# Router in column tiles, choosing experts by rank, first gather from plain rows, bias rows in two rounded passes

## The reference, cut to what matters

```python
scores = softmax(xt @ w_router + b_router)             # first block
grp = scores.reshape(-1, 4, 4)
g_sel = argmax(sum(top_k(grp, 2)))                     # best group by its two best experts
top_w, top_i = top_k(grp[g_sel], 2)
top_w = top_w / sum(top_w)
y = sum_e gate[:, e] * ((silu(xt @ w_gate[e]) * (xt @ w_up[e])) @ w_down[e])
# second block: aff = sigmoid(h @ router_w); the choice is made on aff + router_b,
# the two weights are aff[chosen] / sum(aff[chosen])
```

## Time and profile before

| | |
|---|---|
| runs | 1913.51, 1915.91, 1916.86 us (median 1915.91) |
| profiled execution | 1918.07 us, span from the first to the last instruction 1916.3 us |
| PE | 1750.4 us busy, 91% of the span |
| DVE, ACT | 771.9 us (40%), 403.3 us (21%) |
| weight transfers by SP | 500.20 MB, 299 GB/s read over the span |
| granted TensorE clock, mean | 0.948 of 2.4 GHz |
| chain that ended last | PE 72%, DMA 15%, DVE 7% |

### The profile page before, as it was taken

How to read it: one execution, slowest core, us unless ns; L and a number is a source line. 1 busy time by engine, 2 the same in 40 slices (tenths; PEclk the granted TensorE clock), 3 DMA queues, 4 the chain that set the end, 5 groups by cost and what they waited for, 6 DMA issues and landing times.

```text
span 1916.3 us, 21027 instructions
## 1 busy us (share of the span) xinstructions
PE 1750.4 (91%) x8248; PEld 1032.9 (54%) x8248; DVE 771.9 (40%) x1684; ACT 403.3 (21%) x760; POOL 87.6 (5%) x136
## 2 busy tenths in 40 slices
PE   8999989989799998899897999799998888899995
PEld 4587754433457777544336876544443664654342
DVE  1688631211356766222116356431221654412223
ACT  1232221111022232111103454111110441111111
POOL 1112000000110110000000000000000100000000
PEclk9999969999899998899998999799999899699998
DMA  9868569999974866599995512387999642388995
GB/s 378 338 242 324 220 213 417 421 422 421 421 304 150 316 250 258 230 422 421 421 424 205 215 50 95 126 325 285 421 421 423 241 167 89 150 342 342 421 421 242
DMA packets 82317, 574.46 MB, mean 300 GB/s; under 512 B 8736, under 2 KB 12832, under 8 KB 26912
## 3 DMA queue, kind: packets, MB, share of 16 engines
q1 hardware_dynamic: 60624, 500.20, 64.3%
q0 software_dynamic: 15264, 59.78, 8.4%
q10 hardware_dynamic: 6320, 12.99, 1.9%
HBM read 569.78 MB, written 3.15 MB: 299 GB/s over the span
## 4 chain that ended last, share of the span: by engine, by line
PE 72%; DMA 15%; DVE 7%; issue 3%; ACT 2%; SPq 0%; POOL 0%; POOLq 0%; ACTq 0%; DVEq 0%
PE bank L747 70%; DMA ring<-in_weights 11%; DMA hi_ring<-in_weights 3%; PE bank L779 2%; DVE work L1779 1%; DVE mix L1921 1%; ACT work L1370 1%; DMA consts<-in_cst 1%; DVE mix L1779 1%; DVE small L1779 1%; ACT mix L1370 0%; PE bank L875 0%; DVE oT L1957 0%; DVE small L1930 0%; ACT xT L1370 0%
## 5 line engine op out<-in xcount | busy, mean ns | idle before, releaser
L747 PE MATMUL bank<-ring,work 128*64 128x512 f32 (+2 forms) x1516 | 390.6, 584 | 24.5 <-DMA ring<-in_weights 23.1
L1370 ACT ACTIVATE work<-bank 128x512 f32<-128x512 f32 (+8 forms) x227 | 121.8, 538 | 866.8 <-PE bank L747 467.3
L747 PEld LDWEIGHTS bank<-ring,work 128*64 128x64 f32 (+2 forms) x1516 | 141.5, 144 | 253.4 <-issue 244.0
L747 PE MATMUL bank<-ring,oT 128*64 128x512 f32 (+1 forms) x864 | 228.7, 615 | 8.2 <-DMA ring<-in_weights 7.9
L1779 DVE TENSOR_TENSOR work_parts<-bank,work_parts 128x512 fp32r<-128x512 f32 x68 | 47.0, 692 | 371.8 <-ACT work_parts L1370 371.8
L747 PE MATMUL bank<-hi_ring,work 128*64 128x512 f32 (+1 forms) x608 | 154.3, 596 | 7.5 <-DMA hi_ring<-in_weights 6.0
L747 PEld LDWEIGHTS bank<-ring,oT 128*64 128x64 f32 (+1 forms) x864 | 77.9, 149 | 141.7 <-issue 141.6
L747 PE MATMUL bank<-work_parts 128*128 128x512 f32 (+2 forms) x592 | 147.7, 359 | 5.0 <-DVE work_parts L1779 5.0
L2121 DVE SCALAR_TENSOR_TENSOR work<-bank,small,work 128x512 f32<-128x512 f32 x34 | 25.5, 751 | 308.5 <-PE bank L747 244.4
L747 PE MATMUL bank<-ring,xT 128*128 128x512 f32 (+2 forms) x352 | 138.0, 550 | 1.8 <-DVE xT L2260 1.8
L747 PEld LDWEIGHTS bank<-work_parts 128*128 128x128 f32 x592 | 104.7, 204 | 54.4 <-issue 38.6
(11 more groups left out here) (233 smaller groups left out, 2170.3 us busy)
## 6 DMA issues: line engine op xcount, KB each, us to landing
ring<-in_weights SPq DMA_DIRECT2D x244, 1024.0 KB, 15.1
hi_ring<-in_weights SPq DMA_DIRECT2D x118, 1024.0 KB, 16.2
ring<-in_weights SPq DMA_DIRECT2D x52, 2048.0 KB, 10.2
hi_ring<-in_ada POOLq DMA_DIRECT2D x38, 512.0 KB, 11.4
mod_rows<-in_ada POOLq DMA_DIRECT2D x25, 512.0 KB, 5.9
work<-in_ada POOLq DMA_DIRECT2D x22, 512.0 KB, 6.4
hi_ring<-in_weights SPq DMA_DIRECT2D x5, 2048.0 KB, 10.6
work<-in_vecs POOLq DMA_DIRECT2D x8, 1024.0 KB, 6.4
```

What stands on the lines that cost most here:

```text
L747: ins = nc.tensor.matmul(o, lhsT, rhs, start=start, stop=stop)
L1370: return nc.scalar.activation(o, i, f, **kw)
```

## The change

Five edits:

- **Router.** The logits are computed the other way round: 32 columns of weights (16 and 16 zeros) fixed, 256 columns of `xT` moving, four column tiles side by side (`o[rows, 0:S]`, chunk c in tile c % 4). ACT copies the bank to `router_sums`, and two plain products with `stack` add the four partial sums and turn them. The weights of layers `e` and `o` are loaded over the first ones by a DMA of ACT in layer `1`. In `e` and `o` ACT takes the exponential straight from the bank, and `gate_rows` moves behind `gate_up("u", 0)`.
- **Choosing experts.** All pairs within a group are compared at once (128 elements a row): an expert's rank is how many of its group beat it. The softmax isn't normalised, since only ratios are used.
- **Ranks in rounded form.** `r_in`, `before` and `ones` are rounded (0, 1 are exact), so that the rank products are one record each; the totals are a product of their own, `count`, read by DVE after `picks(0)`.
- **First gather from plain rows.** `gather(0)` takes plain `x` (or `mix`) and plain `pick`: 16 plain products in place of 32 rounded ones. `src_low` moves behind `gathered(0)` and `positions`; `places(0)` moves behind `gate(0)`; ACT's `scaled` moves behind the exponential.
- **Bias rows** are 16 rounded products (table in a high and a low part) in place of 8 plain ones; DVE makes the parts before the cross-attention of layer 0.

```diff
@@ PE, experts @@
-                every = cs("ones")[:, 0:1].broadcast_to([P, P])
+                every = ones_parts[:, 0:1].broadcast_to([P, P])
                 product(f"{tag}.rank", [
-                    (0, NEXP, P, [(cs("before"), r_in[:, 0, :])]),
-                    (NEXP, 2 * NEXP, P, [(every, r_in[:, 0, :]), (cs("before"), r_in[:, 1, :])]),
-                    (2 * NEXP, 3 * NEXP, P, [(every, r_in[:, T, :]) for T in range(NT)])])
+                    (0, NEXP, P, [(before_parts, r_in[:, 0, :])]),
+                    (NEXP, 2 * NEXP, P, [(every, r_in[:, 0, :]), (before_parts, r_in[:, 1, :])])])
+                product(f"{tag}.count", [(0, NEXP, P, [(every, r_in[:, T, :]) for T in range(NT)])])
@@ PE, gather @@
-                                        [(src[:, T, (c0 + c) * P:(c0 + c + 1) * P], pick_parts[:, T, 0:width])
-                                         for src in (src_hi, src_lo(tag)) for T in range(NT)]) for c in range(per)])
+                                        [(src[:, T, (c0 + c) * P:(c0 + c + 1) * P], to[:, T, 0:width])
+                                         for src in rows for T in range(NT)]) for c in range(per)])
...
                 gather(0)
+                gate(0)
                 places(0)
-                gate(0)
                 gate_up("u", 0)
+                if between:
+                    between()
                 gather(1)
@@ PE, bias_rows @@
-                    product(f"row.{h}", [(0, UROW, P, [(pr("rel_table")[0:33, h:h + 1].broadcast_to([33, P]),
-                                                        cs("onehot")[0:33, :])])])
+                    product(f"row.{h}", [(0, UROW, P, [(rel_parts[0:33, k, h:h + 1].broadcast_to([33, P]), onehot_parts[0:33, :])
+                                                       for k in range(2)])])
@@ PE, route @@
-                wr = pr(weights, DC, 16)
-                product(name, [(T * 16, (T + 1) * 16, P, [(xT[:, c, T * P:(T + 1) * P], wr[:, c, :])
-                                                         for c in range(DC)]) for T in range(NT)])
+                wr = pr("router", DC, 32)
+                o = begin(f"{tag}.part")
+                for c in range(DC):
+                    rows = slice(32 * (c % 4), 32 * (c % 4 + 1))
+                    ins = mm(o[rows, 0:S], wr[:, c, :], xT[:, c, :], c < 4, c >= 4)
+                end(f"{tag}.part", ins)
+                ready(f"{tag}.part")
+                product(f"{tag}.logits", [(T * 16, (T + 1) * 16, P, [(router_sums[:, T * P:(T + 1) * P], cs("stack"))])
+                                          for T in range(NT)])
@@ layers e and o (PE; ACT alike) @@
-            route("e.logits", "router_w_2")
-            gate_rows("e.gf", sm("modc", 2, 48)[:, 0, 40:48])
-            experts("e.moe")
+            route("e")
+            experts("e.moe", lambda: gate_rows("e.gf", sm("modc", 2, 48)[:, 0, 40:48]))
@@ ACT @@
                 turned(turn)
+                whole(router_sums, f"{tag[0]}.part")
                 src_high(tag, 1, NT * n + 2)
-            act.wait_ge(router_in, 3)
-            fn(rA, rA, ACT.Exp, scale=-1.0).then_inc(router_exp, 1)
+            whole(ro("A"), "e.logits", ACT.Exp, scale=-1.0)
@@ DVE, route: the thirty small steps become @@
+                other, own = (four.unsqueeze(k).broadcast_to([P, 8, 4, 4]) for k in (2, 3))
+                step.later(tt(r_beats, other, own, ALU.is_gt))
+                step(tt(r_equal, other, own, ALU.is_equal))
+                step(tt(r_equal, r_equal, cs("earlier", 4, 4).unsqueeze(1).broadcast_to([P, 8, 4, 4]), ALU.mult))
+                step(tt(r_beats, r_beats, r_equal, ALU.add))
+                step(v.tensor_reduce(r_rank, r_beats, AX.X, ALU.add))
+                step(v.scalar_tensor_tensor(out=r_top, in0=r_rank, scalar=1.5, in1=four, op0=ALU.is_lt, op1=ALU.mult))
+                step(v.tensor_reduce(r_score.rearrange("p t g -> p (t g)"), r_top, AX.X, ALU.add))
+                step(v.tensor_reduce(r2a, r_score, AX.X, ALU.max))
+                step(tt(r_g, r_score, r2a.unsqueeze(2).broadcast_to([P, 2, 4]), ALU.is_equal))
+                step(tt(r_g, r_g, cs("rank4").unsqueeze(1).broadcast_to([P, 2, 4]), ALU.mult))
+                step(v.tensor_reduce(r2a, r_g, AX.X, ALU.max))
+                step(tt(r_g, r_g, r2a.unsqueeze(2).broadcast_to([P, 2, 4]), ALU.is_equal))
+                v.scalar_tensor_tensor(
+                    out=r_in.rearrange("p t (g j) -> p (t g) j", g=4), in0=r_rank, scalar=1.5,
+                    in1=r_g.rearrange("p t g -> p (t g)").unsqueeze(2).broadcast_to([P, 8, 4]),
+                    op0=ALU.is_lt, op1=ALU.mult).then_inc(group_ready, 1)
@@ DVE, experts @@
-                    for dest in (pick_parts, pick):
+                    for dest in (pick_parts, pick) if j else (pick,):
...
                 picks(0)
+                p_ = bank(f"{tag}.count")
+                drained(f"{tag}.count", v.tensor_copy(sm("counts"), p_[:, 0:NEXP]))
                 gathered(0)
                 if tag[0] in SORTED:
                     positions(tag)
+                src_low(tag)
```

More of the change, by code:

```diff
@@ L180 @@
     ("valid", NT), ("causal", NT * S), ("cos", NT * 32), ("sin", NT * 32), ("onehot", UROW),
-    ("lncount", 2 * NT * 33), ("before", P), ("iota", P), ("ones", 2), ("half", 16), ("tie", NEXP), ("third", NEXP)])
+    ("lncount", 2 * NT * 33), ("before", P), ("iota", P), ("ones", 2), ("half", 16), ("tie", NEXP), ("third", NEXP),
+    ("stack", NEXP), ("earlier", 16)])
 PARAM, PARAM_N = layout([
-    ("w_alow", 2 * DC * 16), ("w_router", DC * 16), ("router_w_2", DC * 16),
+    ("w_alow", 2 * DC * 16), ("router", DC * 32),
     ("b_s", 8), ("w_s", 2 * 4 * P), ("w_a2", 2 * 256), ("norm_mix", 2 * DC),
@@ L248, in constants @@
     put("third", np.tile(3 * e, (P, 1)))
+    put("stack", p[:, None] % 32 == e[None, :])
+    put("earlier", np.tile((np.arange(4)[None, :] < np.arange(4)[:, None]).reshape(-1), (P, 1)))
     return c
@@ L396, in src_lo @@
             return x_as_parts[:, :, :] if tag[0] in "01" else mix_parts[:, :, :]
-        gtmp = cut(work, EX + 3456, 256)
+        gtmp = cut(work, EX + 3456, 512)
         aS = cut(mix[:, :, :].rearrange("p a b -> p (a b)"), 0, 2, 2, S)
@@ L1358, in _ @@
             turn_rows("o.turn1", mix, 3)
-            route("o.logits", "router_w_2")
-            gate_rows("o.gf", sm("modc", 2, 48)[:, 1, 40:48])
-            experts("o.moe")
+            route("o")
+            experts("o.moe", lambda: gate_rows("o.gf", sm("modc", 2, 48)[:, 1, 40:48]))
             assert taken[0] == NPIECES, taken[0]
@@ L1749, in _ @@
             turned_and_split("o.moe", "o.turn1", 3)
-            act.wait_ge(router_in, 4)
-            fn(rA, rA, ACT.Exp, scale=-1.0).then_inc(router_exp, 1)
-            ffn_gate("o.gf")
-            experts("o.moe")
+            whole(ro("A"), "o.logits", ACT.Exp, scale=-1.0)
+            experts("o.moe", lambda: ffn_gate("o.gf"))
             squares(3, range(NT))
@@ L1972, in route @@
             def route(tag, bname, first):
-                p_ = bank(f"{tag}.logits")
-                lg = p_[:, 0:32].rearrange("p (t e) -> p t e", t=2)
+                v.tensor_copy(before_parts, cs("before"))
+                v.tensor_copy(ones_parts, cs("ones"))
                 if first:
+                    p_ = bank(f"{tag}.logits")
+                    lg = p_[:, 0:32].rearrange("p (t e) -> p t e", t=2)
                     drained(f"{tag}.logits", tt(rA, lg, pr("b_router").unsqueeze(1).broadcast_to([P, 2, 16]), ALU.add))
```

110 lines of the change are left out of this document (42 added, 68 removed).

## The result

The changed kernel takes 1881.96 us (median of 1880.26 to 1882.97, four runs), the kernel before 1916.12 (four runs beside it): ratio 0.9823, 95% interval 0.9806 to 0.984. The profiled execution took 1882.8 us, its span is 1881.0 in place of 1916.3, 35.3 us less. The forecast was 1875, alone 1868 to 1882, and with its likelier rivals 1867 to 1889. So direction and range held, the result just inside the narrower one, and 7 us of the forecast gain didn't come. Most of them are missing in layer 0, and most of those at one wait.

The account below looks back on a forecast made before the run. Each expert layer was taken to end one weight stream after its first ring release; gains of 12.4 (layer 0), 11.2 (1), 8.0 (e) and 9.5 (o) sum to 41.1 us, from 1918.07 to 1877, median 1875; range alone 1868 to 1882.

Parts of the forecast that it names:

- its likelier rivals: Clock does not rise before the gates (14%, 1888.5 us); router's column tiles don't all overlap (8%, 1882 to 1895).
- What bounds the kernel: Expert layers end one weight stream after the first ring release; bringing it forward a microsecond ends the layer a microsecond earlier.
- Logits: Router: part product on four column tiles, copy and addition take 3.6 us; 3.5 us saved, 1.9 in layer 0.
- The rival of a stall when the tiles change: Router's part products: switching column tiles stalls PE, making the kernel slower, 1923 us at 1.5 us per product; 3%.
- the estimate in proportion to it: Router's part product: four tiles give 3.2 times, so 2.1 us instead of 1.7, the sum 1.8 us smaller.
- Choice: Choice of experts, logits to rank product: 13 steps for 31, 3.15 us for 6.0; 2.85 saved, 2.8 in e and o.
- Ranks, picks and counts: Rank products to DVE's reading: 1.0 us for 2.43, 1.4 saved; the counts' copy leaves the path, 0.1 saved.
- Places: Places moved from between gather and gate to behind `gate(0)`: 0.25 us saved ahead of the gate.
- The clock: Plain gather brings full clock after about 4 us: 1.4 us saved per gather, gates 2.55, 1.7, 1.2 and 2.7.
- Layer 0: First load 12.4 us earlier: 10.5 from the picks' chain, less 2 for the stores, plus 1.4 and 2.55 from the clock.
- the bias edit: Layer 0's bias rows as 16 rounded products: router starts 4.0 us earlier, less 2 us waiting for the eighth store.
- Layers e and o: 8.0 and 9.5 us gained, after giving back 1.9 for `gate_rows` and 0.6 to 0.7 for places, no longer hidden.

Follow-up runs that it names:

- late_wait: The changed kernel with layer 0's waits for the bias stores moved behind the first gathered rows (DVE) and ahead of the first silu (ACT): 1874.37 us, 0.9792.
- the old logits: The changed kernel with the logits computed as before the change, 32 records into one bank, no sums, no copy: 1892.04 us, 0.9871.
- gather_rounded: The changed kernel with the first gather as 32 rounded products again, low part of the rows left out: 1891.72 us, 0.988.
- bias_plain: The changed kernel with the bias rows as eight plain products again: 1877.97 us, 0.9804.
- rows_early: The kernel of `late_wait` with `gate_rows` of layers e and o back between logits and ranks: 1869.74 us, 0.9767.
- hold_loads: The changed kernel with SP waiting for the eight bias stores before issuing layer 0's first six weight pieces: 1888.97 us, 0.9858.

## Why the prediction was right, and where it was not

- *What bounds the kernel*: right. A microsecond at the first load was a microsecond at the end: 7.06 us there gave 7.4 in `late_wait`; for the old logits 10.8 was expected, and 10.1 measured between the medians (9 by the ratios).
- *Logits*: 3.6 saved in layer 1 (forecast 3.5), 3.5 us of new length for 3.6 forecast. The part product took 1.93 us (1.7 taken). The rival of a stall when the tiles change didn't come: PE starts the logits' addition at 752.97, 0.05 us after ACT's copy ends. The Trainium skill, "TensorE: Matmul & The Clock Gate", part on packing small matmuls, has the speedup of 2.38 for three column tiles; the estimate in proportion to it, 2.1 us, is as near as mine.
- *Choice*: 3.20 us against 3.15 forecast. *Ranks, picks and counts*: 1.67 saved (1.5). *Places* behind the gate: 0.12 gained of the 0.25 in layer 1, and 0.24 lost in layer 0, since PE starts the gate 0.9 to 1.25 us behind the gather whatever stands between.
- *The clock*: the rise came in all four layers. The gates gained their full terms: 2.57, 1.66, 1.26 and 2.67, forecast 2.55, 1.7, 1.2 and 2.7. The gathers gained 0.5, 1.7, 1.0 and 1.0, not 1.4 each: the rise came at 2 x length - 7.09 us, that is 6.1, 3.7, 5.1 and 5.0 us into them, 5 on average where I had taken 4. `gather_rounded` shows that the form of the products does it.
- *Layer 0*: the step that was mis-sized is the stall of DVE on the eight stores, "I take 2 us lost", bounds 0 to 5. It was 6.66. The sum had 12.4 us at the first load and 6.9 came: 4.7 of the 5.5 missing are this wait, 0.9 the gather's clock, 0.5 the pause before the gate, and the chain to the picks was 0.5 better than forecast. Of the store's landing I had counted 9.0 us plus, at most, half of the weights' 15 us. It took 17.84, that is 9.2 more than the 8.6 that it takes alone, or as long as 3.8 MB take at 411 GB/s, of the 6 MB issued about it. The forecast had seen the earlier release and undersized it: the bias edit (forecast +4, less 2) cost about 3.5 us in sum (`bias_plain`), because it sent the weights out ahead of the stores.
- *Layers e and o*: 3.1 and 2.3 us given back after the release, 2.6 forecast; for layer e that is more than the prediction allowed. `gate_rows` costs 2.05 there, and `rows_early` shows that this was to be had.
- The Trainium skill, "DMA: Bandwidth & Descriptors", the part on queues, rings and completion order, says that a DMA engine goes round in turn between the queues that have work, a packet at a time. The runs agree in direction: with six loads of 1 MB on SP's queue, ACT's store of 256 KB took 17.84 us instead of 8.0 to 8.6. An even turn would have served the store earlier, if the packets were alike; no run here shows their order.

## What to carry to other kernels

An edit that makes an engine faster also moves what the engine releases. Before booking the gain, list what the earlier release sends out (here 6 MB of weights) and who has a small transfer under way at that time (here eight stores, whose landing nobody had waited for). The cheap cure is to wait where the buffer is first overwritten, not at the head of the stage: two waits moved, 7 us.

Pauses in a weight stream may be filled or moved, but loads that run ahead of the pause are the stream's lead; holding 12 MB back made the kernel 6 us slower in spite of the picks' 7, holding 6 MB cost nothing.

## What the runs showed of the chip

- 128-column plain products brought the clock from 0.50 to 1.00 within the gather in every layer of the changed kernel (3.7 to 6.1 us into it); rounded ones of the same size, 32 in 7.09 us, in none. Plain products with 16 moving columns, 7.0 us long, didn't either.
- The granted clock fell in the midst of unbroken gathers (`rows_early`, 1203.78 to 1207, 0.60, behind 2.4 us with 0.73 of work), so a record at half clock says little of what PE does at that moment. What exactly decides stays open: the same code had gathers of 3.8 and 6.8 us in two layers. The Trainium skill, "TensorE: Matmul & The Clock Gate", Part 1, says that the number of slow products at the start differs between runs of one kernel; the traces agree, as the starts of layers 1 and e show (the same products at 0.77 to 1.00 in three kernels of this case, and at 0.69 and 0.83 in two).
- Eight stores of 256 KB, issued one in a microsecond, landed in 2.7 to 9.1 us with no weights issued after them (`hold_loads`; 1 MB of vectors was loaded beside them): they fall behind their issue, the last three by 8.5 to 9.1. In the changed kernel the four stores issued before the first weight load (243.87) landed in 2.9 to 5.0 us, the four behind it in 11.4, 13.5, 15.6 and 17.8.
